# Front attention as one unrolled pipeline over eight heads, with another order of tiles and of key groups

## The reference

```
s = einsum('bqhjd,bkhjd->bhjqk', q, k) * A_DK**-0.5      # two score maps j = 0, 1 for each of 8 heads
s = s - slope[h] * |q_pos - k_pos|, masked where k_pos // 64 > q_pos // 64
a = softmax(s);   w = a[:, :, 0] - lam * a[:, :, 1]
o = einsum('bhqk,bkhd->bqhd', w, v)
```

## Time and profile before

| | us |
|---|---|
| median of 3 runs | 4531.06 (4523.66 to 4533.31) |
| the profiled execution | 4518.48 |
| its span in the trace | 4516.9 |
| mean granted TensorE clock, share of full | 0.909 |

### The profile page before, as it was taken

The page is one execution under the profiler, slowest core; times in us unless marked ns, Lnnn a source line. Parts: engine busy times, 40 slices in busy tenths (PEclk is TensorE's granted clock), DMA queues, the critical chain, the costliest instruction groups (busy, mean ns, idle before and its releaser), DMA issues.

```text
span 4516.9 us, 52832 instructions
## 1 busy us (share of the span) xinstructions
PE 3665.5 (81%) x16970; PEld 2141.4 (47%) x16970; DVE 2820.2 (62%) x6369; ACT 1734.6 (38%) x5030; POOL 1522.4 (34%) x1390
## 2 busy tenths in 40 slices
PE   8999999999879887768788588886667676677568
PEld 7998778999557643424333134352222222223112
DVE  4553216776552586667888666666577676676774
ACT  3221113465550133235666332233334444444443
POOL 1110003333110144344444434344444444444442
PEclk9999999999889989978999799998788888889879
DMA  3333224665356699999999999999999999999996
GB/s 117 99 96 115 91 77 150 202 198 160 119 171 215 245 372 418 401 421 409 411 405 396 418 400 362 405 406 421 420 419 398 418 415 416 406 420 403 422 419 258
DMA packets 321093, 1413.24 MB, mean 313 GB/s; under 512 B 39344, under 2 KB 115136, under 8 KB 185664
## 3 DMA queue, kind: packets, MB, share of 16 engines
q0 software_dynamic: 167728, 1166.48, 63.8%
q1 hardware_dynamic: 153104, 243.54, 15.8%
HBM read 1324.55 MB, written 85.35 MB: 312 GB/s over the span
## 4 chain that ended last, share of the span: by engine, by line
DMA 25%; PE 25%; DVE 8%; issue 4%; ACT 4%; POOL 3%; ACTq 0%; DVEq 0%; POOLq 0%
DMA peer_uv<-in_peer_uv_dram,peer_idx 25%; PE peer_acc L3122 12%; PE peer_fo L3026 5%; POOL peer_uv L2097 3%; PE peer_fo L3039 3%; PE peer_fo L2926 3%; DVE peer_uv L2250 2%; PE peer_tb L2870 1%; DVE early L2250 1%; ACT peer_scaled L2628 1%; ACT peer_space L2724 1%; PE peer_fo L3052 1%; DMA early<-in_peer_uv_dram,peer_idx 1%; ACT L2623 1%; POOL early L2097 1%
## 5 line engine op out<-in xcount | busy, mean ns | idle before, releaser
L2250 DVE CUSTOM_DVE_ANT_0 peer_uv<-peer_uv,peer_rep 128x1024 f32<-128x1024 f32 x792 | 964.9, 1225 | 735.3 <-DMA peer_uv<-in_peer_uv_dram,peer_idx 707.9
L2097 POOL DMA_INDIRECT peer_uv<-in_peer_uv_dram,peer_idx x792 | 937.4, 1184 | 1257.5 <-PE peer_acc L3122 1046.9
L3122 PE MATMUL peer_acc<-peer_uv,peer_scaled 128*64 128x512 f32 (+1 forms) x3168 | 941.9, 710 | 434.4 <-ACT peer_scaled L2628 418.0
L2623 ACT ACTIVATE peer_ge<-peer_pre 128x1 f32<-128x1 f32 x1056 | 212.7, 201 | 1542.3 <-DVE peer_pre L2250 1541.1
L3122 PEld LDWEIGHTS peer_acc<-peer_uv,peer_scaled 128*64 128x64 f32 (+1 forms) x3168 | 227.1, 153 | 1021.9 <-ACT peer_scaled L2628 597.3
L3122 PE MATMUL peer_acc<-early,peer_scaled 128*64 128x512 f32 (+1 forms) x1056 | 330.1, 742 | 207.1 <-ACT peer_scaled L2628 201.6
L2097 POOL DMA_INDIRECT early<-in_peer_uv_dram,peer_idx x264 | 301.8, 1143 | 462.0 <-PE peer_acc L3122 419.6
L3026 PE MATMUL peer_fo<-peer_space 128*128 128x256 f32 (+2 forms) x1152 | 393.0, 489 | 50.7 <-DVE peer_space L2304 21.2
L100 PE MATMUL proj_bank<-proj_hTh,proj_wplead 128*128 128x352 f32 x1232 | 426.7, 346 | 1.8 <-DVE proj_wprest L92 1.8
L2628 ACT ACTIVATE peer_scaled<-peer_eased,peer_ge 128x64 f32<-128x64 f32 (+1 forms) x1056 | 366.5, 347 | 122.5 <-ACT peer_ge L2623 3.1
L102 PE MATMUL proj_bank<-proj_hTh,proj_wprest 128*128 128x352 f32 x1232 | 398.2, 323 | 0.0
(11 more groups left out here) (408 smaller groups left out, 5529.2 us busy)
## 6 DMA issues: line engine op xcount, KB each, us to landing
early<-in_w_in_dram POOLq DMA_DIRECT2D x13, 2048.0 KB, 9.4
peer_space<-in_w_ssm_o_dram SPq DMA_DIRECT2D x48, 512.0 KB, 7.9
proj_scan<-scratch_acum SPq DMA_DIRECT2D x36, 512.0 KB, 4.8
early<-in_w_in_dram POOLq DMA_DIRECT2D x14, 1024.0 KB, 8.9
peer_uv<-in_peer_uv_dram,peer_idx POOLq DMA_INDIRECT x792, 12.5
peer_space<-in_w_attn_o_dram SPq DMA_DIRECT2D x24, 512.0 KB, 8.6
peer_space<-in_w_out_dram SPq DMA_DIRECT2D x24, 512.0 KB, 7.9
scratch_xtok<-proj_shared SPq DMA_DIRECT2D x20, 512.0 KB, 2.9
```

Source lines behind the costliest of these rows:

```text
L2097: pool.indirect_dma_start(uv[k][:], None, io["peer_uv"], bass.IndirectOffsetOnAxis(ap=idx[t % 2][:, col:col + 1], axis=0)).then_inc(uv_in[ ...
L2250: dve.tensor_tensor_reduce(uv[k][:, 0:D], uv[k][:, 0:D], rep[j][:], 1.0, 0.0, ALU.mult, ALU.add, pre[:, k:k + 1]).then_inc(u_done, 1)
L2623: act.activation(ge[:, k:k + 1], pre[:, k:k + 1], ACT.Gelu_apprx_tanh).then_inc(gelu_done, 1)
L3122: x = pe.matmul(acc[group(t, slot % groups_of(t)), h:h + HALF], scaled[slot][:, 0:r], uv[slot][:, D + h:D + h + HALF], start=(it == 0 and ...
```

## The change

It replaces the four trips by one straight pipeline of 48 steps for all eight heads, so the pipeline fills and empties once. The order of a head's tiles becomes 0, 2, 4, sample, 3, 1. The keys of a head are no longer turned and copied in one lump before it: in the head's first four steps one group each follows the weights, in the order 3, 0, 1, 2. All values waited for are constants, and `hold`'s increments go from this stage. POOL's loads keep their conditions; `head_used` is raised after the head's last tile, now tile 1. The last head's stores of attention rows change places, and the last halving of `negdist` goes. The matmuls, the shapes and the stores are the same.

```diff
-    ORDER = EARLY + (SAMPLE,)
+    ORDER = (0, 2, 4, SAMPLE, 3, 1)
+    KEYS = (3, 0, 1, 2)
     NTILES = len(ORDER)
-    STEPS = 2 * NTILES
+    STEPS = H * NTILES
...
+    jobs = []
+    for m in range(STEPS + 1):
+        if m:
+            jobs += [("w", m - 1, g) for g in range(len(groups(tile_of(m - 1))))]
+        if m < STEPS and m % NTILES < 4:
+            jobs.append(("k", m // NTILES, KEYS[m % NTILES]))
...
+                for h in range(2, H):
+                    b = h % 2
+                    pool.wait_ge(head_used[b], h // 2)
+                    load_head(pool, b, h * P)
+                    pool.wait_ge(stored[b], (h // 2 + 1) * 80)
+                    values_of(pool, b, h * P)
...
-                with sp.Fori(0, H // 2 - 1) as i:
-                    for b in range(2):
-                        store(i, b, i * (2 * P) + b * P)
+                for h in range(H - 2):
+                    store(h)
                 load_ahead(sp)
-                store(H // 2 - 1, 0, (H - 2) * P)
...
+                store(H - 2)
...
-                with dve.Fori(0, H // 2) as i:
-                    for m in range(STEPS + 1):
-                        if m < STEPS:
-                            bias_and_max(i, m)
-                        if m % NTILES == NTILES - 1:
-
-                            dve.tensor_scalar(negdist[:], negdist[:], 0.5, None, ALU.mult).then_inc(slope_done, 1)
-                        if m:
-                            combine(i, m - 1)
+                for m in range(STEPS + 1):
+                    if m < STEPS:
+                        bias_and_max(m)
+                    if m < STEPS - 1 and m % NTILES == NTILES - 1:
+
+                        dve.tensor_scalar(negdist[:], negdist[:], 0.5, None, ALU.mult).then_inc(slope_done, 1)
+                    if m:
+                        combine(m - 1)
...
-                with act.Fori(0, H // 2) as i:
-                    keys_out(i, 0)
-                    for m in range(STEPS + 2):
-                        if m < STEPS:
-                            exps(i, m)
-                        if m == NTILES - 1:
-                            keys_out(i, 1)
-                        if m >= 2:
-                            o_to_rows(i, m - 2)
-                        if 1 <= m <= STEPS:
-                            weights_out(i, m - 1)
+                for m in range(STEPS + 2):
+                    if m < STEPS:
+                        exps(m)
+                    if m >= 2:
+                        o_to_rows(m - 2)
+                    if 1 <= m <= STEPS:
+                        weights_out(m - 1)
+                    if m < STEPS and m % NTILES < 4:
+                        keys_out(m // NTILES, KEYS[m % NTILES])
...
+                scores(0)
+                for m in range(STEPS + 2):
+                    if m + 1 < STEPS:
+                        scores(m + 1)
+                    if m >= 2:
+                        product(m - 2)
+                    if 1 <= m <= STEPS:
+                        weights_turned(m - 1)
+                    if m < STEPS and m % NTILES < 4:
+                        keys_turned(m // NTILES, KEYS[m % NTILES])
```

More of the change, by code:

```diff
@@ L1246, in differential_attention, with turn_val @@
         inv_done, scaled, w_done, slope_done = s.sem("inv_done"), s.sem("scaled"), s.sem("w_done"), s.sem("slope_done")
[L1247 to L1255, removed]
+        turned, turn_out, o_done, o_out = s.sems("turned", 2), s.sems("turn_out", 2), s.sem("o_done"), s.sem("o_out")
+        def turn_val(j, ahead=1):
+            return j // 2 + ahead
         def load_head(eng, b, col):
@@ L1405, in weights_out @@
                         j = turn_of["w", m, g]
-                        act.wait_ge(turned[j % 2], turn_val(i, j))
-                        act.wait_ge(o_done, step_of(i, m, 2))
+                        act.wait_ge(turned[j % 2], turn_val(j))
+                        act.wait_ge(o_done, m + 2)
                         full = [q for q in blocks if q[1] == P]
@@ L1476, in scores, with keys_turned @@
-                def scores(i, m):
-                    b, n = m // NTILES, tile_of(m)
+                def keys_turned(h, g):
+                    b, j = h % 2, turn_of["k", h, g]
+                    out = tp[j % 2]
+                    pe.wait_ge(turn_out[j % 2], turn_val(j))
+                    if g < 2:
+                        for k in range(4):
+                            t = pe.transpose(out[:, k, :], kT[b][:, (4 * g + k) * P:(4 * g + k + 1) * P], c.ident[:])
+                    elif g == 2:
+                        t = pe.transpose(out[0:DEC, 0, :], kT[b][:, SEQ:T], c.ident[:])
+                    else:
+                        for k in range(KC):
+                            t = pe.transpose(out[:, k, :], kc[b][:, k, :], c.ident[:])
+                    t.then_inc(turned[j % 2], 1)
@@ L1478, in scores @@
+                def scores(m):
+                    h, n = m // NTILES, tile_of(m)
+                    b = h % 2
+                    if m == 0:
+                        pe.wait_ge(c.head_in, 48)
+                    elif m % NTILES == 0:
+                        pe.wait_ge(head_in[b], (h + 1) // 2 * 48)
                     for j in range(2):
-                        hold(pe, pe_gate, biased[j], step_of(i, m))
+                        pe.wait_ge(biased[j], m + 1)
                         half = slice(AK * j, AK * j + AK)
@@ L1517, in product @@
                         j = turn_of["w", m, g]
-                        hold(pe, pe_gate, turn_out[j % 2], turn_val(i, j, 2))
+                        pe.wait_ge(turn_out[j % 2], turn_val(j, 2))
                         for k, (blk, size) in enumerate(blocks):
```

145 lines of the change are left out of this document (49 added, 96 removed).

## The result

| | before | after |
|---|---|---|
| median of the runs (same chip) | 4528.19 us (4 runs, 4523.66 to 4533.31) | 4479.91 us (4 runs, 4478.07 to 4483.44) |
| ratio to before, 95% interval | | 0.9899 [0.9887, 0.9912] |
| profiled execution | 4518.48 us, span 4516.9 | 4478.14 us, span 4476.4 |
| stage: end of the last projection matmul to the last output copy | 195.53 us | 149.29 us |
| from one sixth bias pass to the next, by head | 19.37 and 28.38 in turn | 16.92, 16.92, 16.93, 16.92, 17.18, 16.76, 17.84 |

A forecast was written before the change was run, and what follows sets the result against it. The front attention stage was taken to pay for a drain, lumped keys and a slow clock. 1160.7 + (14.4 - 1.3 + 5) + 7 x 17.7 + 5.2 = 1307.9 against 1347.3, -39.4 us: 4491 us, range 4479 to 4509.

The forecast's parts named there:

- First bias pass: Stage start: with keys no longer first, it starts about 1160.0 instead of 1161.03, 1.0 us gained, and ends at 1160.7.
- First head: First of the stage's eight heads: 14.4 less 1.3 for the missing combine plus 5 us (3 to 8) for low clock.
- Seven spacings: Heads after the first: seven periods of 17.7 us, with bounds 16.75 (DVE alone) and 19.4.
- the recurrence: Steady head worked step by step for PE and DVE: 0.89 us lost at tile 4, 0.29 at tile 2, period 17.9.
- Gates: Removed gate increments on PE, 30 per head, 1.5 us; given 0.2 a head (0 to 1.5), most under running matmuls.
- Tail: Stage end, from the end of the last bias pass to that of the last copy: about 5.2 us, before 7.45.
- The load floor of 17.7: POOL's loads land 9.0 us after a head's last copy, PE offers 9.3; period at least 9.0 + 8.6 + 0.1.
- A: PE's gates cost all 1.5 us and loads land earlier; DVE alone decides, 16.8 a head: 4483 us; chance 0.10.
- B: Loads gate the head, landing 2 us later; period 19.8 in six heads: 4504 us; chance 0.18.
- D: Next stage waits for a weight or row load no earlier, losing the gain; gain 0 to 15: 4524 us; chance 0.06.
- C: Clock stays low in the stage as short PE waits recur; PE's 17.9 becomes 28.6: 4571 us; chance 0.04.
- The cross-check: Stage gain: gaps 30, key lumps 10, start and end 3, slow heads 9, less coupling 8, first-head clock 2: 42 us.

## Why the prediction was right, and where its sizes were off

**The cause** was as told: the stage paid for drains, for a lump of keys and for a slow clock behind them, and time saved there moved everything behind it. The experiments show the first two by putting them back; the clock's own share in the kernel before wasn't measured apart. The place of the gain (stage 46.2 us shorter), the single table load, the clock (1.00 from 1168, told "from about 1175") and DVE's only wait, before tile 4, are in the profile. DVE had no wait before the first tile of any head from the second on; at the last head PE waited 1.19 for q, which DVE felt one step later.

**The sum** had 147.2 us from the first bias end to the last copy; the trace has 140.5. Term by term:

- First bias pass: forecast 8.9 us after the last projection matmul, measured 8.8.
- First head: forecast 18.1, measured 14.6. A steady head takes 14.2 over the same stretch and the missing combine takes 1.3 off, so the slow clock cost about 1.7 and not 5 (bounds given: 3 to 8, and it fell below them). The row with 1127 ns came from heads that stayed slow for nearly their whole length; here the clock was back some 4 us after the first bias pass. The 14.6 is also on the short side: other executions with the same work had 15.2 to 15.3.
- Seven spacings: forecast 17.7 each, 123.9; measured 119.5, a mean of 17.07. This is the term that was mis-sized most, 4.4 us. Two steps failed in it. The tile 4 score group was entered with 1.93, less overlap 1.86; its row held a wait between the two halves of the tile, and the group holds PE for 1.29. With it the recurrence put the next PE start 3.24 later, where it is 2.48, and PE arrived 0.67 late at tile 2, where it is on time: the forecast waits of 0.89 and 0.29 were 0.52 and 0. And DVE's head without waits was 16.40, not 16.75: six hand-overs take 0.05 less each, and with the gates put back they were 0.17 again. It came as near as that only because 0.17 beside POOL's issue is in it, which the forecast didn't have. DVE had 12 gates a head too, and the forecast priced PE's alone.
- Gates: 0.2 a head forecast, 0.29 in a steady head by putting them back (the stage lost 4.2 us in all, in one run).
- Tail: forecast 5.2, measured 6.4. DVE waits 0.91 for an output copy there (at 1299.98), which I had not in the list.

Sum of the misses: 3.5 + 4.4 - 1.2 = 6.7 us. By the profiled pair the forecast was 4479.1, and the execution took 4478.14: the 2.8 us ahead of the stage and the 2.9 behind it took most of the 6.7 back, and that is chance. By the medians, 4491 against 4479.9, the median of before is 2.9 lower in the runs beside the result, and 1.5 to 2 are left that no row assigns. The measured median lies 0.9 us above the lower end of the range, and two of its four runs (4478.07 and 4478.14) lie below it. So the mechanism was right and the sizes were too large by nearly the whole width of the range on that side.

**The load floor of 17.7** was too high. The floor assumed that q would land 9.0 after the last copy and be wanted at 9.3. It landed 8.4 after it (1203.75 + 7.2 against 1202.53), since POOL's issue came 0.05 before the copy's end and not up to 0.47 behind it, and PE wanted it about 9.4 after. The slack was 1.0 us here. In the other heads q took 7.6 to 8.0 us to land in place of 7.2, and the slack was 0.2 to 0.6, at the last head, with 8.5, it was gone. So there was a floor, and at a spacing of 16.92 the kernel stood close to it.

**The rivals.** A gave the number nearest to the result (4483, 16.8 a head) but for the wrong reason: gates that cost 0.29 and not 1.5, and a wait that is smaller, not absent. B (the loads gate each head) happened at one head of seven, with 0.2 us of slack at two others. D did not happen. C did not happen in this kernel: the clock held 1.00 with a short wait in each head. The Trainium skill (TensorE: Matmul & The Clock Gate, "A second HAM failure mode: psum-queue depth-cycling") describes a clock that swings under small frequent gaps; this kernel's traces don't show that, as there were such gaps in every head and the clock stayed at 2.4 GHz. What the late loads showed is a clock at 1.2 GHz for some 6.8 us with four of six longer waits, of 1.39 us and up, and at 2.4 GHz with the other two. Rival C was thus nearer in this kernel than its 4 in 100: with one step's delay of an increment it comes about in four heads.

**The cross-check** by gaps (three drains 30 us, four lumps 10, start and end 3, slow heads 9, less coupling) came near the result, but the experiments don't bear out its parts: a drain alone costs 3.5 us, and the lump, in step with the others, 12.5 in all. What was counted as one drain of 10 us is drain, lump and clock together. That its total of 42 is near the measured 46.2 is luck in the parts.

What stays open: why the clock came back earlier in the first head of 14.6 us than in those of 15.2 to 15.3 with the same work, and what in POOL's issue delays DVE. What tips the clock behind a wait of PE is open too. Nor was it isolated why the clock held through the drains put into the changed kernel and fell in those of the kernel with the loops written out: the lump of keys, the order and the length of the gap differ between them at once.

## What to carry to other kernels

Where two engines pass work to and fro, write down the one engine's own time per period and then its waits beyond the normal hand-over, one by one; here 16.40 plus the waits gave the spacing of four other kernels within 0.1 us (with every delay counted, from 16.23, it came to 17.76 for a measured 17.77), and each edit is then a question of which waits it removes. Before a group's duration goes into such a recurrence, see in the timeline whether a wait is inside it. And when tiles are put in another order, list all partners of a step (scores ahead, product behind, copy that frees the buffer): an order that pairs two of them well can be worse by the third.

## What the runs showed of the hardware that was not expected

- The same kind of wait of PE for a load was followed by a granted clock of 0.50 (1.2 GHz) in some heads and not in others. With the loads released late: it fell with waits of 1.39, 1.54, 1.59 and 5.93 us, for some 6.8 us each time, and held with 1.46 and 1.91. With the gates put back it held with 1.61, in the changed kernel with 1.19; with large and small tiles in turn it fell with 1.70. It held through the drains put into the changed kernel, with PE busy 1.14 of 2 us. A wait of some 1.5 us of PE thus cost 1.2 to 1.7 us a head where the clock held and 4.4 where it fell.
- Score matmuls overlap in the records: four with 512 columns, at a mean of 641 ns each 2.56 us, and four with 128 columns hold PE for 1.29 us together (1200.12 to 1201.41). A mean of one can't be multiplied by the count there; the start of the next group can be read.
- Four trips of a hardware loop over five engines cost 5.3 us of the stage against the same code written out (four table loads on ACT, one of 1.28 us in each trip, against one), although the clock fell twice more in the code written out.
- 42 waits with an increment behind them cost 0.29 us in a steady head, though PE's 30 alone sum to 1.5 us by the earlier trace rows: four fifths lay under running work.
- A small instruction of DVE (negative maximum of 128x2, 0.17 us) took up to 0.44 us when POOL was issuing a load, and ended within 0.03 us of the end of the issue, in all six heads of the changed kernel in which it was stretched. It moved the next step by 0.17 in the steady heads.
